# Moving two more of r's projection tiles into the seven-product slots, and the mixer pieces re-planned for 44 half tiles

## What is computed

```python
xn   = rmsnorm(x, norm1_g)
proj = xn @ w_in                      # 2048 -> q, k (512 each), v, r (1024 each), a_lr (16), cb, cc, ch, cu, cv (512 each)
loga = log_sigmoid(a_lr @ w_a2 + b_a) / 16
o    = gla_chunked(q * DK**-0.5, k, v, loga, S0)     # exp(cumsum(loga)) scales q and k, chunks of 64
o_gla  = rms-normalised(o) * gla_g * silu(r)
o_conv = cb * (conv_b + sum_j conv_w[j] * shifted(cc * ch))
o_cm   = gelu(cu) * (tril(cm_ws) @ layernorm(gelu(cv)) + cm_bs)
h = x + concat[o_gla, o_conv, o_cm] @ w_out
y = h + (silu(rmsnorm(h) @ w_gate) * (rmsnorm(h) @ w_up)) @ w_down
```

## Time and profile before

| | |
|---|---|
| median of 3 runs | 2176.32 us (2176.09 to 2176.43) |
| the profiled execution, its own time | 2176.26 us |
| its span, from the first to the last instruction | 2174.5 us |
| TensorE (PE) busy | 2163.6 us, 99% |
| VectorE (DVE) busy | 1707.6 us, 79% |
| ScalarE (ACT) busy | 1014.1 us, 47% |
| granted TensorE clock over the span | 0.999 |

### The profile page before, as it was taken

How to read it: one execution, slowest core, us unless ns; L and a number is a source line. 1 busy time by engine, 2 the same in 40 slices (tenths; PEclk the granted TensorE clock), 3 DMA queues, 4 the chain that set the end, 5 groups by cost and what they waited for, 6 DMA issues and landing times.

```text
span 2174.5 us, 40815 instructions
## 1 busy us (share of the span) xinstructions
PE 2163.6 (99%) x17272; PEld 2158.1 (99%) x17272; DVE 1707.6 (79%) x2004; ACT 1014.1 (47%) x1352; POOL 11.5 (1%) x16
## 2 busy tenths in 40 slices
PE   9999999999999999999999999999999999999998
PEld 9999999999999999999999999999999999999998
DVE  7766567655686799888888888888888888887887
ACT  8333352315454555444444544444454445444455
POOL 0000000000000000000000000000000000000001
PEclk9999999999999999999999999999999999999999
DMA  5332233327333434344445444444544885555523
GB/s 192 105 120 86 92 107 117 108 86 259 109 107 108 148 127 156 124 152 159 142 138 162 142 132 155 154 134 142 159 150 157 297 301 213 191 201 189 208 87 133
DMA packets 123024, 328.90 MB, mean 151 GB/s; under 512 B 10863, under 2 KB 51375, under 8 KB 121745
## 3 DMA queue, kind: packets, MB, share of 16 engines
q1 hardware_dynamic: 122368, 327.10, 44.9%
q10 hardware_dynamic: 528, 0.07, 0.0%
HBM read 269.39 MB, written 57.74 MB: 150 GB/s over the span
## 4 chain that ended last, share of the span: by engine, by line
PE 96%; DVE 2%; ACT 1%; issue 1%; DMA 0%; POOL 0%; POOLq 0%; SPq 0%; DVEq 0%; ACTq 0%
PE acc L1729 24%; PE acc L1409 19%; PE g L1729 18%; PE acc L1737 12%; PE g L1737 9%; PE acc L1638 3%; PE g L1638 2%; PE acc L1676 2%; PE g L1676 2%; PE g L1630 1%; PE acc L1630 1%; DVE w_lo L2512 1%; PE g L1436 0%; PE g L1578 0%; DVE w_s L2537 0%
## 5 line engine op out<-in xcount | busy, mean ns | idle before, releaser
L1214 ACT CAST w_hi<-w_s 128x1024 fp32r<-128x1024 f32 (+1 forms) x204 | 209.1, 1025 | 358.0 <-DVE w_s L2537 349.1
L1729 PE MATMUL g<-op_hi,w_hi 128*128 128x272 f32 x1056 | 272.1, 288 | 0.0
L1729 PE MATMUL acc<-sg_hi,w_hi 128*128 128x272 f32 x1056 | 272.1, 288 | 0.0
L1729 PE MATMUL g<-op_lo,w_hi 128*128 128x272 f32 x1056 | 271.9, 288 | 0.0
L1729 PE MATMUL acc<-op_hi,w_hi 128*128 128x272 f32 x1056 | 271.6, 289 | 0.2 <-ACT acc L1184 0.2
L1729 PE MATMUL acc<-sg_lo,w_hi 128*128 128x272 f32 x1056 | 271.4, 288 | 0.0
L1729 PE MATMUL acc<-op_lo,w_hi 128*128 128x272 f32 x1056 | 271.4, 288 | 0.0
L2512 DVE TENSOR_TENSOR w_lo<-w_s,w_hi 128x1024 fp32r<-128x1024 f32 (+1 forms) x204 | 242.7, 1190 | 12.6 <-ACT w_hi L1214 7.0
L1409 PE MATMUL acc<-op_hi,w_hi 128*128 128x272 f32 x1152 | 241.6, 291 | 0.2
L1409 PE MATMUL acc<-op_hi,w_lo 128*128 128x272 f32 x1152 | 238.3, 288 | 0.0
L1409 PE MATMUL acc<-op_lo,w_hi 128*128 128x272 f32 x1152 | 238.3, 288 | 0.0
(11 more groups left out here) (395 smaller groups left out, 4883.2 us busy)
## 6 DMA issues: line engine op xcount, KB each, us to landing
w<-w_gu SPq DMA_DIRECT2D x88, 512.0 KB, 3.3
w_raw<-w_gu SPq DMA_DIRECT2D x88, 512.0 KB, 4.1
w_raw<-w_in SPq DMA_DIRECT2D x55, 512.0 KB, 3.5
hf_dram<-hf_hi SPq DMA_DIRECT2D x22, 952.0 KB, 6.4
hf_dram<-hf_lo SPq DMA_DIRECT2D x22, 952.0 KB, 8.7
w_raw<-w_d SPq DMA_DIRECT2D x34, 512.0 KB, 4.0
w<-w_d SPq DMA_DIRECT2D x26, 512.0 KB, 3.3
op_hi<-hf_dram SPq DMA_DIRECT2D x16, 544.0 KB, 7.0
```

The lines of the kernel that those rows point to most:

```text
L1214: nc.scalar.copy(w_hi[:, (C_ST + n) % RING, 0:w], src[:, 0:w]).then_inc(hi_ready, 1)
L1729: nc.tensor.matmul(out, w_h, x, start=fresh and j == 0 and i == 0, stop=False, skip_group_check=True)
```

## The change

Six of r's tiles go through slots instead of four: `NR` is 3 and there are nine slots. Two r tiles stay classical, so the third stage has 44 half tiles (h0 to h43) instead of 48. The heads whose r is made early are 1, 2 and 3, and their normalisation comes first. All pieces from `z` 1 on move: `b` goes from a distance of two half tiles to one and a half, and everything behind it comes three to four and a half half tiles earlier. `conv_tile` stays where the convolution tiles are, at h11, h17, h23 and h29. The round trip of r through DRAM carries six tiles instead of four, and x comes back in two transfers early and two late instead of three and one.

```diff
-T_Q, T_CV, T_CONV, T_CU, T_R, N_IN = 1, 17, 21, 33, 37, 41
+T_Q, T_CV, T_CONV, T_CU, T_R, N_IN = 1, 17, 21, 33, 37, 39
...
-NR = 2
+NR = 3
...
-HEAD_ORDER = (2, 3, 0, 1)
+HEAD_ORDER = (2, 3, 1, 0)
...
-Z_AT = (C_T + 3, C_T + 6)
-B_AT = tuple(C_T + 5 + 2 * i for i in range(5))
-KDT_AT = C_T + 15
-QS_AT = tuple(C_T + 17 + i for i in range(8))
-MU_AT, VAR_CM_AT, VVT_AT, ZC_AT = C_T + 19.5, C_T + 21.5, C_T + 26, (C_T + 27, C_T + 28)
-S_AT = (C_T + 23, C_T + 25) + tuple(C_T + i for i in (29.5, 30.5, 31.5, 32.5, 33.5, 35, 36, 37.5))
-P_AT = tuple(C_T + 29 + i for i in range(4))
-OSQ_AT = C_T + 32
-ON_AT = tuple(C_T + i for i in (34, 36.5, 38, 40))
+Z_AT = (C_T + 3, C_T + 7)
+B_AT = tuple(C_T + i for i in (5, 6.5, 8, 9.5, 11))
+KDT_AT = C_T + 12.5
+QS_AT = tuple(C_T + 14 + i for i in range(8))
+MU_AT, VAR_CM_AT, VVT_AT, ZC_AT = C_T + 16.5, C_T + 18.5, C_T + 23, (C_T + 24, C_T + 25)
+S_AT = (C_T + 20, C_T + 22) + tuple(C_T + i for i in (26.5, 27.5, 28.5, 29.5, 30.5, 32, 33, 34.5))
+P_AT = tuple(C_T + 26 + i for i in range(4))
+OSQ_AT = C_T + 29
+ON_AT = tuple(C_T + i for i in (31, 32.5, 34, 35.5))
...
-                if c == C_T + 13:
+                if c == C_T + 14:
...
-                    if c == math.ceil(S_AT[2 + i] + 6.5):
+                    if c == min(math.ceil(S_AT[2 + i] + 6.5), C_OUT - 4):
                         store_s0(i)
...
-                    for i in range(3):
+                    for i in range(2):
                         sp.dma_start(trunk[:, 4 * i:4 * i + 4, :], xT[:, 4 * i:4 * i + 4, :]).then_inc(x_back, 16)
...
                 if c == C_OUT - 1:
                     sp.wait_ge(front_done, 2 * NR)
-                    sp.dma_start(trunk[:, 12:, :], xT[:, 12:, :]).then_inc(x_back, 16)
+                    for i in (2, 3):
+                        sp.dma_start(trunk[:, 4 * i:4 * i + 4, :], xT[:, 4 * i:4 * i + 4, :]).then_inc(x_back, 16)
...
                 if c == R_AT + 1:
-                    dve.wait_ge(post_v, parts(V_KINDS, ("on", 1)))
+                    dve.wait_ge(post_v, parts(V_KINDS, ("on", 2)))
```

More of the change, by code:

```diff
@@ L446, in slot_out @@
         def slot_out(s):
-            return kv[:, s + 4 if s < NR else s - NR]
+            return kv[:, s + 6 - NR if s < NR else s - NR]
         def slot_kv(n):
@@ L629, in _ @@
                     load_s0(1)
-                if c == C_T + 14:
+                if c == C_T + 15:
                     sp.wait_ge(inter, number(("z", 1)))
@@ L986, in op_hi_tile @@
             def op_hi_tile(k):
-                act.wait_ge(mix_done, k - 3)
+                if k < KT - 2:
+                    act.wait_ge(mix_done, k - 3)
                 act.wait_ge(chunk_done, C_OUT)
@@ L2276, in kv_outputs @@
                 if piece == C11:
-                    if s >= NR + 4:
-                        dve.wait_ge(r_out, 16 * (s - NR - 3))
+                    if s >= 6:
+                        dve.wait_ge(r_out, 16 * (s - 5))
                     nc.vector.tensor_tensor(y[:, 0, 0:TH], pa[:, q, 0:TH], rstd[:, 0:TH], ALU.mult).then_inc(kv_read, 1)
@@ L2441, in _ @@
                 if c == R_AT + 1:
-                    dve.wait_ge(post_v, parts(V_KINDS, ("on", 1)))
+                    dve.wait_ge(post_v, parts(V_KINDS, ("on", 2)))
                     for i in range(2 * NR):
                         dve.wait_ge(r_act, i + 1)
-                        nc.vector.tensor_tensor(mix[:, 4 + i, :], mix[:, 4 + i, :], trunk[:, KT - 2 * NR + i, :],
-                                                ALU.mult).then_inc(front_done, 1)
+                        m = mix[:, KT // 2 - 2 * NR + i, :]
+                        nc.vector.tensor_tensor(m, m, trunk[:, KT - 2 * NR + i, :], ALU.mult).then_inc(front_done, 1)
                 if c == MIX_SINGLE_AT:
```

## The result

The changed kernel takes 2184.91 us (median of 5, 2183.78 to 2185.66), the kernel before 2176.32 us: **+8.6 us, ratio 1.0038 (1.0027 to 1.0049)**. The prediction was 2179.6 us in a range that ended at 2183.5.

A forecast was written before the change was run, and what follows sets the result against it. TensorE, busy 99% of the span, was taken as the bound, so removed matmuls gain and new waits add in full: -2.3 + 4.7 + 0.9 = +3.3 us on 2176.3, giving 2179.6 us, range 2176.5 to 2183.5.

The forecast's parts named there:

- Matmuls, -2.3 us: TensorE's work: four half tiles fewer (24.1 us) against one more slot (21.8 us), net -2.3 us.
- The wait ahead of `b` 2, +4.7 us: Third stage: `b` 2 waits for `z` 1's part, a 14.1 us chain against 9.4 us of TensorE work, +4.7 us.
- `mu`, `conv_tile` and `qs` 4, +0.9 us: Third stage: `qs` 4 waits for query blocks behind `mu`'s part and `conv_tile` on VectorE, 11.1 against 10.2 us, +0.9 us.
- the clock in that one case fell just when mine would end: Argument against a clock loss at `b` 2: at program end the clock fell 4.6 to 4.7 us after idleness began.
- rival 1: The wait ahead of `b` 2 also lowers TensorE's clock, 2.3 us more: 2181.9 us; chance 0.31.
- there was room of more than one half tile: Output projection: its operands, formed a little later, still come in time; priced at nothing.
- entries at the start of the output projection: Sign: TensorE waits there would show the covers priced at nothing wrong.
- Rival 3: A tight cover fails too (`b` 1's, `vvt`, S0 reloads, late x): 1 to 3 us more, about 2181.6; chance 0.09.
- Rival 4: Each ScalarE table switch costs its 1.28 us load again, twice in `b` 2's chain: 2182.2 us; chance 0.03.

The follow-up runs named there:

- r two half tiles sooner: The changed kernel with r's Silus behind h34 and its products at h35 (`R_AT` C_T + 34 instead of C_T + 36): 2182.14 us.
- `b` 2 later: The changed kernel with `b` 2, `b` 3 and `b` 4 half a half tile later (8.5, 10, 11.5): 2180.87 us.
- the kernel with all three edits: The changed kernel with `z` 1 behind h4, `R_AT` at C_T + 35 and `mu` behind h16: 2183.47 us.
- mu sooner: The changed kernel with `mu` behind h16 instead of in the middle of h17: 2183.91 us.

## Why the prediction was wrong

Point by point, by its own terms, against the profiled execution (+9.4 us):

- **Matmuls, -2.3 us: right.** The ninth slot costs 21.77 us, four half tiles are 24.08, and in the changed kernel's trace the sum over the stages closes to 0.1 us.
- **The wait ahead of `b` 2, +4.7 us: right**, 4.8, with the chain and the releaser as read.
- **`mu`, `conv_tile` and `qs` 4, +0.9 us: right in its mechanism**, 1.25 us measured. VectorE's three pieces ended 11.4 us behind `mu` (394.96 to 406.38) and not 11.1:

```profile
395.36 2.62 DVE L2056 SCALAR_TENSOR_TENSOR mix<-g,mix 128x544 f32<-128x544 f32 x4 [1.38 <-PE g L1463]
...
401.09 0.72 DVE L1939 TENSOR_TENSOR tmp<-acc,rstd 128x544 f32<-128x544 f32 x1
...
406.19 0.19 DVE L1976 TENSOR_TENSOR qm<-trunk,qm 128x32 fp32r<-128x32 f32 x1
```

- **The first failed step: "the clock in that one case fell just when mine would end."** From one row, a fall 4.6 us behind the last matmul, I took a point at which to decide and gave rival 1 only 0.31. That row was one draw from a wide spread: at the end of the program the clock fell between 2.2 and 5.1 us behind the last matmul in the fourteen traces, and in the eight with a wait of 3.7 us or more it fell every time, 2.5 to 4.2 us behind the last matmul ahead of the wait. What the clock costs I had right in size, 2.3 us forecast and 2.3 in this execution, but partly by luck: the forecast took it from the program's first matmuls, where the earlier trace rows show a granted clock of 1.00 in both windows and only the pace doubles (219 ns a matmul, then 109), and the traces with a long wait lost 1.3 to 2.7 us. Rival 1 by itself would have been 2181.9.
- **The second failed step: "there was room of more than one half tile" behind the operands of the output projection**, priced at nothing: it cost 2.8 us. No row stood behind that half tile; I had looked at the two tiles of r that are left, not at VectorE's queue. Before, `op_lo` for the third product ended at 595.46 and TensorE asked some 6.6 us behind 591.49, at 598.1: a room of 2.6 us, less than half of a half tile. The lateness, 4.0 us at this instruction, follows on 2.6 us at `mix_forms`; what added the 1.4 us between the two isn't traced. That the products of r, left in place, start it is shown by the one run that moves them alone to a free place: r two half tiles sooner has `mix_forms` at 25.8 us again and a projection of 85.2 us. And I had followed the pieces that the change moved, not the one that it left in place: `R_AT` stayed while the end of the stage came to it. The last line of the section on what would show it named this sign, "entries at the start of the output projection".
- **Rival 3** had the right price for one failed cover (1 to 3 us) and named the late x transfers, not the products; it should have been added to rival 1 and not set beside it. The range was said to leave out the upper parts of rivals 3 and 4, but its end, 2183.5, lies above either (2182.6 and 2182.2); what it left out were two losses at once. By the rows: 2176.3 - 2.3 + 4.8 + 2.3 + 1.25 + 2.8 + 0.5 of scatter = 2185.7, the profiled execution.
- **Rival 4, table switches that cost double: no.** In the changed kernel too the next activation starts 0.01 us behind the load (325.40 + 1.28 = 326.68, then 326.69). The 2.8 us that the Trainium skill, "ScalarE: Activation LUTs", "What ACT_TABLE_LOAD costs", would have added do not exist here, and that the measured +8.6 lies nearer to the +6.1 which I worked out from that page than to my +3.3 is chance.

## What to carry to other kernels

When a stage gets shorter, list every step whose place is counted from its start and stays, next to the steps that are counted from its end: those two now meet. Measure the room of a result on the queue of the engine that makes it, from its end to the moment that its reader asks, and not by counting tiles between two places. And where the bounding engine is TensorE, price a long wait with its clock: in these traces each wait of 3.7 us or more brought 1.3 to 2.7 us of half-rate work on top, those up to 1.8 us none, and between the two nothing was tried.

## What the runs showed of the hardware

Waits are counted here from the start that was due, which makes them some 0.15 us longer than the entries. The granted clock never fell in waits of 1.3 to 1.8 us (`qs` 4, `b` 2 later, the output projection). It fell in all eight waits from 3.7 us on; in the two of 3.7 us only when TensorE had started again (at 300.26, with `z` 1 at 299.96, and in the kernel with all three edits 0.7 us behind the start). Waits between 1.8 and 3.7 us weren't tried; at the end of the program the clock fell as early as 2.2 us behind the last matmul. The same wait of 4.8 us at the same instruction was followed by 6.8 us at the lower level in four traces and by 3.4 us in one (mu sooner), a loss of 2.3 to 2.7 us or of 1.3; with a wait of 7.8 us the low stretch was 10.2 us and the loss 2.3. So the loss differs from execution to execution of the same instructions, and it should be entered as a range. The Trainium skill, "TensorE: Matmul & The Clock Gate", Part 1, says that how many matmuls run cold at a kernel's start differs from run to run of the same kernel; these traces show the like behind a wait, in kernels that are the same up to there, with one trace of each.
